# First modulation tiles as four 2 MB transfers into free memory, with the first projection interleaved on halves of the features

## The reference, cut to what matters

```python
ml = [m[:, None, :] for m in jnp.split(jax.nn.silu(c) @ ada_w[layer] + ada_b[layer], N_MOD, axis=-1)]
mc = jnp.split(jax.nn.silu(c_ctx) @ ada_w[layer] + ada_b[layer], N_MOD, axis=-1)
a_lat = modulate(rms_norm(h_lat, norm1_w[layer]), ml[0], ml[1])     # h * (1 + scale) + shift
a_ctx = modulate(rms_norm(h_ctx, norm1_w[layer]), mc[0], mc[1])
...
mla_attend(q, k, v): s = einsum('bhqd,bhkd->bhqk', q, k) * MLA_QK ** -0.5; p = softmax(s); p @ v
```

## Time and profile before

| | before |
|---|---|
| three runs, median | 1944.23 us (1941.6 to 1945.97) |
| profiled execution, its own time | 1942.06 us |
| its span in the trace | 1940.3 us |
| PE busy, share of the span | 1835.3 us, 95% |
| DVE / ACT / POOL busy | 1230.4 / 928.6 / 154.6 us |
| mean granted clock of PE | 0.976 of full |
| moved by DMA | 256.52 MB, mean 132 GB/s |

### The profile page before, as it was taken

The page is one execution under the profiler, slowest core; times in us unless marked ns, Lnnn a source line. Parts: engine busy times, 40 slices in busy tenths (PEclk is TensorE's granted clock), DMA queues, the critical chain, the costliest instruction groups (busy, mean ns, idle before and its releaser), DMA issues.

```text
span 1940.3 us, 39187 instructions
## 1 busy us (share of the span) xinstructions
PE 1835.3 (95%) x15552; PEld 1606.2 (83%) x15552; DVE 1230.4 (63%) x2017; ACT 928.6 (48%) x1491; POOL 154.6 (8%) x151
## 2 busy tenths in 40 slices
PE   5999979999999999998999999999899998899997
PEld 2895558788888887887888999998799998689997
DVE  1867765488668667543556776577676647857654
ACT  1433453353123325454444665457566544457653
POOL 0000000200000010004351100100200001020000
PEclk8999987999999999999999999999999999899999
DMA  7653101336555543230003556543356563126553
GB/s 276 225 196 130 64 1 44 135 117 193 165 166 171 178 139 114 81 97 3 4 4 93 170 180 187 180 142 125 112 174 182 175 185 108 35 88 191 184 175 101
DMA packets 73056, 256.52 MB, mean 132 GB/s; under 512 B 7776, under 2 KB 12000, under 8 KB 72288
## 3 DMA queue, kind: packets, MB, share of 16 engines
q1 hardware_dynamic: 72928, 254.69, 41.4%
HBM read 253.61 MB, written 1.05 MB: 131 GB/s over the span
## 4 chain that ended last, share of the span: by engine, by line
PE 85%; DVE 8%; ACT 4%; issue 2%; DMA 1%; SPq 0%; POOL 0%; DVEq 0%; ACTq 0%; POOLq 0%
PE bank L401 23%; PE bank L403 22%; PE bank L402 22%; PE bank L393 2%; DMA ring<-ada_w 1%; PE bank L420 1%; PE bank L2002 1%; PE bank L1011 1%; DVE weights_lo L351 1%; ACT weights_hi L344 1%; DVE h L2629 1%; PE bank L2027 1%; PE bank L2007 1%; DVE a L2627 1%; PE bank L996 1%
## 5 line engine op out<-in xcount | busy, mean ns | idle before, releaser
L401 PE MATMUL bank<-x_hi,weights_hi 128*128 128x256 f32 (+1 forms) x2024 | 642.1, 317 | 27.2 <-DVE x_lo L2585 10.9
L403 PE MATMUL bank<-x_hi,weights_lo 128*128 128x256 f32 (+1 forms) x2024 | 632.6, 313 | 0.0
L402 PE MATMUL bank<-x_lo,weights_hi 128*128 128x256 f32 (+1 forms) x2024 | 632.4, 312 | 0.0
L351 DVE TENSOR_TENSOR weights_lo<-ring,weights_hi 128x1024 fp32r<-128x1024 f32 x376 | 462.0, 1231 | 236.9 <-ACT weights_hi L344 234.3
L344 ACT ACTIVATE weights_hi<-ring 128x1024 fp32r<-128x1024 f32 x376 | 395.2, 1055 | 357.2 <-PE bank L403 354.8
L401 PEld LDWEIGHTS bank<-x_hi,weights_hi 128*128 128x128 f32 x2024 | 386.8, 191 | 60.6 <-issue 22.6
L402 PEld LDWEIGHTS bank<-x_lo,weights_hi 128*128 128x128 f32 x2024 | 387.0, 191 | 23.2 <-issue 1.4
L403 PEld LDWEIGHTS bank<-x_hi,weights_lo 128*128 128x128 f32 x2024 | 386.7, 191 | 22.0
L401 PE MATMUL bank<-hidden_hi,weights_hi 128*128 128x256 f32 (+1 forms) x864 | 271.6, 314 | 0.0
L402 PE MATMUL bank<-hidden_lo,weights_hi 128*128 128x256 f32 (+1 forms) x864 | 271.6, 314 | 0.0
L403 PE MATMUL bank<-hidden_hi,weights_lo 128*128 128x256 f32 (+1 forms) x864 | 271.6, 314 | 0.0
(11 more groups left out here) (377 smaller groups left out, 2277.1 us busy)
## 6 DMA issues: line engine op xcount, KB each, us to landing
ring<-mlp_w SPq DMA_DIRECT2D x128, 512.0 KB, 4.2
ring<-w_ffn_in SPq DMA_DIRECT2D x88, 512.0 KB, 3.5
a<-ada_t SPq DMA_DIRECT2D x32, 512.0 KB, 3.3
mix<-ada_t SPq DMA_DIRECT2D x32, 512.0 KB, 3.9
ring<-w_ffn_out SPq DMA_DIRECT2D x32, 512.0 KB, 3.5
ring<-gdn_w_in SPq DMA_DIRECT2D x24, 512.0 KB, 3.5
ring<-even_w_in SPq DMA_DIRECT2D x18, 512.0 KB, 4.6
ring<-ada_w SPq DMA_DIRECT2D x16, 512.0 KB, 6.4
```

The lines of the kernel that those rows point to most:

```text
L351: nc.vector.tensor_tensor(w_lo[:, g % AHEAD, :], ring[:, g % RAW, :], w_hi[:, g % AHEAD, :].bitcast(F32), ALU.subtract).then_inc(lo_done[g ...
L401: pe.matmul(dst, lhs[0](k), rhs[0](k), start=start and k == 0, stop=False)
L402: pe.matmul(dst, lhs[0](k), rhs[1](k), start=False, stop=False)
L403: last = pe.matmul(dst, lhs[1](k), rhs[0](k), start=False, stop=stop and k == nk - 1)
```

## The change

It does five things.

1. The first 2048 columns of `ada_w[0]` are laid out on the host in four quarters, each 128 x 4096 floats (2 MB, 16 KB per partition). Quarter q holds feature half q // 2 of shift *and* scale, for four of the eight row blocks. So group 0 of `ada_a` now is shift and scale of features 0 to 511, and group 1 that of 512 to 1023.
2. The quarters are loaded by four transfers into `x_hi`, `x_lo`, the first half of `hidden_hi` and the first half of `hidden_lo`, all unused so far (`ada_lands`). The ring now only has tiles that are split, and the second numbering of `Tiles` goes.
3. SP's order: vectors, `xt`, `tab`, quarter 0, even tiles 0 to 2, quarters 1, 2, 3, even tile 3, and on as before.
4. PE's, DVE's and ACT's orders are rewritten: sums first, then group 0 (quarters 0 and 1), its turn, 6 filler products, then the three first blocks for k = 0 to 3 with the tiles of quarters 2 and 3 and the turn of group 1 between, then k = 4 to 7. The weight splits of the first three tiles move ahead of x, and x is made in two halves of four blocks. The 15 filler products go.
5. In the latent attention the scale MQK ** -0.5 goes into the copy of q out of PSUM, and the maximum comes out negated from one instruction (before: a maximum, then a multiplication by -scale).

The signal `mla_here` is merged into `early_here` (16 for quarter 0, 48 with the two later loads), and the counts of `mod_here` start one transfer higher.

```diff
             def __init__(self, n, source, kb=KB, cols=P):
-                self.ring_first = Tiles.landed
...
         def split_hi(act, g, body=None):
-            r = ring_place(g)
-            act.wait_ge(here[r % RAW].sem, after(16 * (r // RAW + 1), body, 16 / RAW))
+            act.wait_ge(here[g % RAW].sem, after(16 * (g // RAW + 1), body, 16 / RAW))
...
-            def dve(self, dve, between=None):
-                dve.wait_ge(gains_done.sem, 2 * self.l + self.which + 1)
+            def dve(self, dve, k0=0, k1=KB, gains=None):
+                dve.wait_ge(gains_done.sem, 2 * self.l + self.which + 2 if gains is None else gains)
                 self.norm.wait(dve)
-                for k in range(KB + 1):
-                    if between is not None and k == FIRST:
-                        between()
-                    if k < KB:
+                for k in range(k0, k1 + 1):
+                    if k < k1:
...
-        ada_a_tiles = ada_tiles(0, 0, ADA_A)
+        QUARTER = 4
+        mod_here = [sig(f"modulation_here{s}") for s in range(3)]
+        early_here = sig("early_here")
+        ada_here = [early_here] + mod_here
+
+        def ada_lands(q):
+            at = (2 * HIDDEN, 2 * HIDDEN + QUARTER * D, 0, HIDDEN)[q]
+            return arena[:, at:at + QUARTER * D]
...
             def pe_tile(self, pe, t):
                 g, k = divmod(t, KB)
-                r = self.tiles.ring_first + t
+                q, i = divmod(t, QUARTER)
                 if t == 0:
                     pe.wait_ge(silu_done.sem, 1)
-                if k == 0 and len(self.banks) == 1:
-                    pe.wait_ge(ada_copied.sem, self.base + g)
-                pe.wait_ge(here[r % RAW].sem, 16 * (r // RAW + 1))
-                w = ring[:, r % RAW, :]
+                if i == 0:
+                    pe.wait_ge(ada_here[q].sem, 16)
+                w = ada_lands(q)[:, i * D:(i + 1) * D]
...
+        def dve_first_ada(dve, g):
+            dve.wait_ge(ada_turned.sem, ada_a.base + g + 1)
+            n = KB // 2
+            for part in range(2):
+                dve_bias(dve, 0, part * KB + g * n, n, ada_columns(0, g * KB + part * n, n).rearrange("p (j z) -> p j z", z=2))
+            dve_gain(dve, 0, 0, g * n, n)
...
-        def pe_begin(pe):
-            for t in range(2 * KB):
-                if t == KB:
-                    pe.wait_ge(loaded.sem, 16 * SMALL)
-                    n1.norm.pe_sums(pe)
-                if t == KB + 3:
-                    ada_a.pe_turn(pe, 0)
-                ada_a.pe_tile(pe, t)
-            ada_a.pe_turn(pe, 1)
...
+        def pe_first_blocks(pe, k0, k1):
+            if k0 == 0:
+                for n in range(FIRST):
+                    even_tiles.wait(pe, n)
+                    even_lin.free(pe, n)
+            last = split_products(pe, [even_lin.bank(n)[:, :] for n in range(FIRST)], [even_tiles.parts(n) for n in range(FIRST)],
+                                  split_x(T), KB, lambda k: n1.ready(pe, k), range(k0, k1))
+            if k1 == KB:
+                for ins in last:
+                    ins.then_inc(block_done.sem, UNITS)
+
+        def pe_ada(pe, q):
+            for t in range(q * QUARTER, (q + 1) * QUARTER):
+                ada_a.pe_tile(pe, t)
+
+        def pe_begin(pe):
+            pe.wait_ge(loaded.sem, 16 * SMALL)
+            n1.norm.pe_sums(pe)
+            pe_ada(pe, 0)
+            pe_ada(pe, 1)
+            ada_a.pe_turn(pe, 0)
+            keep_busy(pe, 3, 6)
+            pe_first_blocks(pe, 0, 1)
+            pe_ada(pe, 2)
+            pe_first_blocks(pe, 1, 2)
+            pe_ada(pe, 3)
+            pe_first_blocks(pe, 2, 3)
+            ada_a.pe_turn(pe, 1)
+            pe_first_blocks(pe, 3, 4)
+
         def pe_even_in(pe):
...
+            pe_first_blocks(pe, KB // 2, KB)
...
-                        ins = nc.scalar.activation(qT[NOPE:MQK, 4 * n + x, :], o[x * ROPE:(x + 1) * ROPE, :], ACT.Copy)
+                        ins = nc.scalar.activation(qT[NOPE:MQK, 4 * n + x, :], o[x * ROPE:(x + 1) * ROPE, :], ACT.Copy,
+                                                   scale=MQK ** -0.5)
...
-                        link(dve, nc.vector.reduce_max(s[:, 0:1], self.scores(i), AX.X))
-                        nc.vector.tensor_scalar(s[:, 1:2], s[:, 0:1], -self.scale, None, ALU.mult).then_inc(att_max.sem, 1)
+                        nc.vector.tensor_reduce(s[:, 1:2], self.scores(i), AX.X, ALU.max, negate=True).then_inc(att_max.sem, 1)
...
             if g.body is None:
                 for t in range(g.n):
-                    if g is ada_a_tiles and t == RAW:
-                        sp.dma_start(h[:, :, :], d["xt"]).then_inc(loaded.sem, 16)
-                        sp.dma_start(tab[:, 0:TURN_AT + TURN_SIZES[0]], d["tab"]).then_inc(loaded.sem, 16)
+                    if g is even_tiles and t == FIRST:
+                        for q in range(1, 4):
+                            sp.dma_start(ada_lands(q), d["ada_w"][q]).then_inc(ada_here[q].sem, 16)
...
             sp.dma_start(vec[:, :], d["vec"]).then_inc(silu_inputs.sem, 16)
+            sp.dma_start(h[:, :, :], d["xt"]).then_inc(loaded.sem, 16)
+            sp.dma_start(tab[:, 0:TURN_AT + TURN_SIZES[0]], d["tab"]).then_inc(loaded.sem, 16)
+            sp.dma_start(ada_lands(0), d["ada_w"][0]).then_inc(ada_here[0].sem, 16)
...
             n1.norm.act_squares(act, arrived)
+            n1.norm.act_root(act)
+            for g in range(FIRST):
+                split_hi(act, g)
             ada_a.act_copy(act, 0)
-            n1.norm.act_root(act)
+            n1.act(act, 0, KB // 2)
             ada_a.act_copy(act, 1)
-            n1.act(act, lambda: [split_hi(act, g) for g in range(FIRST)])
+            n1.act(act, KB // 2, KB)
             split_hi(act, FIRST)
...
             n1.norm.dve_squares(dve, arrived)
-            dve_ada(dve, ada_a.turned(), 0, 0, ADA_A)
-            n1.dve(dve, lambda: [split_lo(dve, g) for g in range(FIRST)])
+            for g in range(FIRST):
+                split_lo(dve, g)
+            dve_first_ada(dve, 0)
+            n1.dve(dve, 0, KB // 2, 1)
+            dve_first_ada(dve, 1)
+            n1.dve(dve, KB // 2, KB, 2)
             split_lo(dve, FIRST)
...
             pe_begin(pe)
-            keep_busy(pe, 7, 15)
             pe_even_in(pe)
...
     ada = np.asarray(inputs["ada_w"])
-    maps["ada_w"] = np.ascontiguousarray(ada[0:1, :, 0:2 * D])
+    first = ada[0, :, 0:2 * D].reshape(2, KB // 2, P, 2, 2, D // 2).transpose(4, 0, 2, 1, 3, 5)
+    maps["ada_w"] = np.ascontiguousarray(first.reshape(4, P, KB // 2 * D))
```

More of the change, by code:

```diff
@@ L328, in after @@
             return body[0] * int(step) + count
-        def ring_place(g):
-            for x in Tiles.every:
-                if not x.unsplit and x.first <= g < x.first + x.n:
-                    return x.ring_first + g - x.first
         def split_hi(act, g, body=None):
@@ L560, in dve, with act @@
                         ins.then_inc(xl_done.sem, 1)
-            def act(self, act, between=None):
-                for k in range(KB):
-                    if between is not None and k == FIRST:
-                        between()
+            def act(self, act, k0=0, k1=KB):
+                for k in range(k0, k1):
                     act.wait_ge(scaled.sem, self.scaled + k + 1)
@@ L651, in two_block_kernel @@
         PER_BODY = 3
-        mod_here = [sig(f"modulation_here{s}") for s in range(PER_BODY)]
+        assert len(mod_here) == PER_BODY
         mod_used = sig("modulation_used")
@@ new lines, in two_block_kernel, with dve_bias, dve_gain @@
+        norm_w = [vector(name).rearrange("p (l k o) -> p l k o", l=2, o=1) for name in ("norm1_w", "norm2_w")]
+        def dve_bias(dve, layer, j0, n, src):
+            bias = ada_bias[:, layer, j0:j0 + n].rearrange("p (j o) -> p j o", o=1).broadcast_to((P, n, 2))
+            link(dve, nc.vector.tensor_tensor(mod[:, layer, j0:j0 + n, :], src, bias, ALU.add))
+        def dve_gain(dve, layer, which, k0, n):
+            j = (3 * which + 1) * KB + k0
+            nc.vector.scalar_tensor_tensor(out=gain[:, layer, which, k0:k0 + n], in0=mod[:, layer, j:j + n, :], scalar=1.0,
+                                           in1=norm_w[which][:, layer, k0:k0 + n].broadcast_to((P, n, 2)),
+                                           op0=ALU.add, op1=ALU.mult).then_inc(gains_done.sem, 1)
@@ new lines, in dve_first_ada, with dve_ada @@
+        def dve_first_ada(dve, g):
[4 more added lines that the diff above has]
+            dve_gain(dve, 0, 0, g * n, n)
+        def dve_ada(dve, layer, j0, n):
+            dve.wait_ge(mod_used.sem, EARLY if layer == 0 else EARLY + LATE)
+            dve_bias(dve, layer, j0, n, mod[:, layer, j0:j0 + n, :])
+            for which in range(2):
+                if j0 <= (3 * which + 1) * KB < j0 + n:
+                    dve_gain(dve, layer, which, 0, KB)
@@ L781, in even_sync @@
             return t, even_tiles.done(t, units - 1 if last else b), units - b if last else 1, last
```

(18 more changed lines are left out.)

90 lines of the change are left out of this document (28 added, 62 removed).

## The result

| | before | after |
|---|---|---|
| median of six runs each, side by side | 1945.10 us (1941.26 to 1953.07) | 1932.41 us (1927.19 to 1934.92) |
| ratio with 95% interval | | 0.9927 [0.9902, 0.9952] |
| profiled execution, its own time | 1942.06 | 1933.5 |
| its span | 1940.3 | 1931.7 |
| mean granted clock of PE | 0.976 | 0.978 |

The change takes 12.7 us off by the medians. The direction and the mechanism were right; the gain was 1.7 times what I gave it by the medians, and 1.9 times by the ratio (14.2 us).

The account below looks back on a forecast made before the run. PE bounds the kernel; only its idle time in the beginning, waiting for ada_w tiles and norm sums, could be won. 9.3 (block n = 4) - 2.1 (clock) + 0.3 (attention) = 7.5 us off, giving 1936.7 us; range 1931 to 1941.

Parts of the forecast that it names:

- clock after it: Behind PE's wait before block n = 4: granted clock falls for some 4.2 us at half pace, costing 2.1 (0 to 4).
- attention: Latent attention: PE sets the pace, so the removed DVE instructions gain only 0.3 us (0 to 4.9).
- Pace of the first 9 us: First transfers: 208 GB/s up to 9 us and 422 after it, so the inputs are here at 12.9.
- Rival 1: First transfers: slow start was the tiles' own; all 2.5 us earlier, 10.0 won, 12.1 without a clock fall; chance 0.14.
- Tiles of 0.64: PE's ada_w work: each tile takes 0.64 us, so a quarter's four take 2.6.
- Fillers and the start: PE before the projection: 12 filler matmuls take 2.6 or 5.1 us; projection starts at 34.5 (33.8 to 35.8).
- DVE's second half: DVE making x of blocks 4 to 7: 0.64 + 2.74 + 3 x 1.6 us after the turn, last x_lo at 54.6.
- The chain behind the last x_lo: Last x_lo to weight tile 4's lo split: 12.5 us, making PE wait 3.7 at block n = 4; 9.3 won.
- 2, the end of the first blocks counting: Projection: the end of the first blocks counts, not the chain behind x_lo; 13.2 us off, 1931.0; chance 0.05.
- 3, a low clock in the beginning: Between sums and fillers the clock falls, slowing tiles, turn and fillers; 1939.7 to 1943.2; chance 0.17 shared with 5.
- 4: Loads: q3 comes too late, at 63.4 if 208 GB/s persists; 12.8 us slower, 1957; chance 0.06.
- 5: Projection starts on half the features but nothing ends sooner; price that of rival 3 at worst; chance 0.17 shared with it.

Follow-up runs that it names:

- b3: The kernel before with DVE's lo split of weight tile 4 moved ahead of early modulation tile 0; 1944.73 us, ratio to before 0.9996.
- x1: The changed kernel with DVE's lo split of weight tile 4 moved ahead of early modulation tile 0; 1929.91 us, ratio to before 0.9917.
- x2: The changed kernel with the old attention put back (maximum, then a multiplication; scale in the exponential); 1935.91 us, ratio to before 0.9942.
- x5: The changed kernel with quarter 0 issued ahead of `xt` and `tab`; 1935.61 us, one run.
- a2_same: The changed kernel run again unedited (the repeat); 1932.76 us, ratio to before 0.9947.
- x3: The changed kernel with each quarter loaded by four transfers of 512 KB instead of one of 2 MB; 1937.57 us, ratio to before 0.9954.
- x6: The changed kernel with quarter 0 first in the queue and every quarter loaded as four transfers of 512 KB; 1932.82 us, one run.
- x4: The changed kernel without the halves: all four quarters and both turns before the projection, x made in one go; 1937.95 us, ratio to before 0.9949.
- x7: As x1, with PE's turn of group 1 moved ahead of the first blocks' k = 2; 1929.75 us, ratio to before 0.9915.

## Why the prediction was wrong in size and right in kind

**The failed step** is the time line of the beginning, from "inputs here at 12.9" to "last x_lo at 54.6": the pace of the first transfers, ada_w's tiles, the start behind the fillers and DVE's second half were each taken too slow, and they add up. The last x_lo ended at 49.42, 5.2 sooner. In the order of the prediction:

| step | predicted | measured |
|---|---|---|
| inputs here (squares start) | 12.9 | 10.68 |
| end of the sums | 22.8 | 20.56 |
| q1 here | 26.6 | 24.34 |
| a quarter's four tiles | 2.6 | 1.93 |
| projection starts | 34.5 (33.8 to 35.8) | 30.91 |
| last x_lo ends | 54.6 | 49.42 |
| from there to tile 4 split and PE on it | 12.5 | 12.9 (12.2 in the repeat) |
| PE's wait for it | 3.7 | 3.14 (2.50 in the repeat) |
| block n = 4 starts | 67.1 | 62.31 |
| clock after it | 2.1 | 1.7, and 0 in the repeat |
| attention | 0.3 | 0.26 |

1. *Pace of the first 9 us.* I took 208 GB/s from a window in which four small tiles headed the queue; with `xt` at the head it is 289. That is 0.73 MB more by 9 us, or 1.7 us at 422 GB/s; the other 0.5 of the 2.2 (inputs) and 2.3 (q1) is my allowance of 1.5 us from the last byte to the engine, which was too long. Rival 1 named just this and priced it at 2.5; its time was right, and 0.14 was too low a chance for it. I carried 208 over to transfers of another size and to another order, and it was a single execution's: b3 has 269 with the order of before. How much of the difference is the size and how much the execution stays open.
2. *Tiles of 0.64.* That row is a lone tile, start to end. In a row of four tiles they start 0.48 apart: 32 instructions in 1.93. The trace of before had three in a row at that pace (below). Three quarters lie on the path to the last x_lo (q1, q2, q3), each 0.67 shorter.
3. *Fillers and the start.* I let them run partly slow and took 34.5, above my own 33.8. They ran at full pace, 2.84, inside DVE's and ACT's time for block 0. That is 0.7.
4. *DVE's second half.* From the turn to the last x_lo I took 8.2 us (0.64 + 2.74 + 3 x 1.6), and it took 7.6 (41.85 to 49.42): the last block has no scaling behind it. That is 0.6.

```profile
32.96 1.50 PE L625 MATMUL bank<-ring,arena 128*32 128x256 f32 x24
```

Up to the start of the projection: 2.3 (q1) + 0.7 (its tiles) + 0.7 (fillers) = 3.7, seen 3.6. Behind it: the interleaving took 10.9 instead of 11.9 us, 1.0 less (two quarters 1.5 shorter, the steps between 0.5 longer), and DVE 0.6 less. Together 5.2. With the measured terms the sum is 14.05 - 1.7 + 0.26 = 12.6 us, and the medians show 12.7. That close a match is luck: the spans of two executions of this kernel differ by 6.1. Where the clock doesn't fall it is 76.36 - 61.74 + 0.26 = 14.9.

**What held.** The chain behind the last x_lo was the next bound. Its length was 12.9 against 12.5 and the wait was in its place; x1 removed it and b3 showed the slack of before. "The wait hardly depends on the beginning" held too: the beginning came 5 us sooner and the wait changed by 0.6 (1.2 in the repeat). The clock fell behind the wait in three of the six profiles that have one of 2.5 to 3.1 us there: after (3.14), x2 (2.9) and x5 (2.51), and not in a2_same (2.50), x3 (2.5) and x6 (3.0). From its start to the marker the block takes 5.8 us without a fall, and 7.4, 8.6 and 7.2 in these three. The term of 2.1 is thus 1.4 to 2.8 in some executions and 0 in others.

**The rivals.** 1 was right on the time (item 1); that the small tiles were the whole reason is not shown. 2, the end of the first blocks counting, is refuted by the 3.14 at L384; x1 shows what it would have brought (its marker is 17.5 us ahead of before's). 3, a low clock in the beginning, didn't occur in either profile of the changed kernel, but did in x4's and x7's. Of the eight profiles with the halves x7's is the only one with a fall there, so with this order it is rare but possible. 4 is refuted: 425 GB/s over 27 us and quarter 3's tiles start at 37.27 without a wait. The Trainium skill (DMA: Bandwidth & Descriptors, Specifications) lists about 358 GB/s for a core, as half of the rate of the HBM stack that two cores share; at that rate behind the first 9 us q1 would be here near 27.5, an estimate, and it was here at 24.34. The 425 of this trace, of one core working alone, decides. 5 is refuted: the last x_lo ends 13.8 us sooner (63.22 to 49.42).

**How firm the number is.** The repeat's 0.9947 [0.9928, 0.9966] holds my forecast of 1936.7 / 1944.23 = 0.9961, the first interval doesn't. What says that 7.5 was too small is the trace: 12.3 and 14.5 us at the marker against my 9.3 - 2.1 = 7.2 (11.5 and 13.7 if b3's 81.21 stands for before).

## What to carry to other kernels

Loads that pass through a small ring take on every delay of their consumer; let the first ones land in memory that is not yet in use, and their size hardly matters. When the start of a stage is moved, follow every chain that hangs on the moved event and had little slack (here 0.6 us), and move whatever in it doesn't need the event: one reordered split was worth 3 us at the marker after the change (the clock aside) and nothing before it. Look also at what stands in the middle of a chain and could be done earlier: three weight splits held the making of x up by 4 us. For a sum, take the pace of repeated work from start to start in a row, not from a lone record, and don't carry a transfer rate from one execution over to another order of the queue.

## What the runs showed of the hardware

- Over the first 9 us the DMA moved 289 to 309 GB/s in nine profiles with a 2 MB transfer at the head of the queue, and 208 (before), 269 (b3) and 243 (x6) in three with four of 512 KB. Before and b3 have the same beginning, so the spread is as large as the difference. Later the size made little: 410 against 425.
- The same program showed low-clock stretches in different places in two executions (63 to 67 and 160 to 172 in one, not in the other) and spans of 1931.7 and 1925.6. The length of the wait at tile 4 didn't decide it: a fall followed 2.51 us (x5) and none 3.0 (x6). A fall there cost 1.4 to 2.8 us.
